# A sub-layer with a gated recurrence and a convolution: the values' projection as a Strassen block product

## What is computed

```
h = rmsnorm(x, pre_norm_g[l])
proj = jnp.einsum('btd,dn->btn', h, w_in[l].astype(h.dtype))
q, fz, iv, gate_a, u, ug, gate_b = jnp.split(proj, split_pts, axis=-1)
o_a = hgrn2_mixer(q, fz, iv, lower_bounds[l], hg_norm_g[l]) * jax.nn.silu(gate_a)
o_b = conformer_conv(u, ug, dw_kernel[l], dw_bias[l], conv_ln_g[l], conv_ln_b[l]) * jax.nn.silu(gate_b)
mixed = jnp.concatenate([o_a, o_b], axis=-1)
y = jnp.einsum('btm,md->btd', mixed, w_out[l].astype(mixed.dtype))
x = x + rmsnorm(y, post_norm_g[l])
```

## Time and profile before

| | |
|---|---|
| median of 3 runs | 869.82 us (869.69 to 869.93) |
| the profiled execution | 869.98 us, of which the span of the page is 868.3 us |
| TensorE busy | 856.2 us, 99% |
| VectorE busy | 628.1 us, 72% |
| ScalarE busy | 413.7 us, 48% |
| GpSimd busy | 330.9 us, 38% |
| moved | 100.27 MB |

### The profile page before, as it was taken

How to read it: one execution, slowest core, us unless ns; L and a number is a source line. 1 busy time by engine, 2 the same in 40 slices (tenths; PEclk the granted TensorE clock), 3 DMA queues, 4 the chain that set the end, 5 groups by cost and what they waited for, 6 DMA issues and landing times.

```text
span 868.3 us, 12325 instructions
## 1 busy us (share of the span) xinstructions
PE 856.2 (99%) x4210; PEld 718.2 (83%) x4210; DVE 628.1 (72%) x1017; ACT 413.7 (48%) x648; POOL 330.9 (38%) x159
## 2 busy tenths in 40 slices
PE   8999999999999999999999999999999999999996
PEld 7988888888888888888888888888888888888885
DVE  4687787787787994775839477583957894686657
ACT  7533313313313465654746466465646843554542
POOL 3294444444444444352442425244342455032100
PEclk9999999999999999999999999999999999999999
DMA  9243333333333323142231313313241246977955
GB/s 309 86 146 97 97 97 97 98 97 97 97 98 97 96 74 97 49 122 73 72 97 52 117 48 99 95 51 104 62 121 48 74 137 210 230 144 158 274 204 194
DMA packets 121342, 100.27 MB, mean 115 GB/s; under 512 B 2992, under 2 KB 101593, under 8 KB 120025
## 3 DMA queue, kind: packets, MB, share of 16 engines
q1 hardware_dynamic: 116201, 86.14, 32.4%
q0 software_dynamic: 4352, 8.39, 5.6%
q10 hardware_dynamic: 752, 5.25, 1.5%
HBM read 95.57 MB, written 4.19 MB: 115 GB/s over the span
## 4 chain that ended last, share of the span: by engine, by line
PE 97%; DMA 1%; ACT 1%; DVE 0%; SPq 0%; DVEq 0%; issue 0%; ACTq 0%
PE banks L1424 19%; PE banks L1422 19%; PE banks L1423 19%; PE banks L1561 3%; PE banks L1560 3%; PE banks L1439 3%; PE banks L1559 3%; PE banks L1438 3%; PE banks L1437 3%; PE banks L1596 3%; PE banks L1595 3%; PE banks L1594 3%; PE banks L1368 3%; PE banks L1480 1%; PE banks L1470 1%; PE banks L1486 1%
## 5 line engine op out<-in xcount | busy, mean ns | idle before, releaser
L426 POOL TENSOR_TENSOR w_lo<-w_raw,w_hi 128x1024 fp32r<-128x1024 f32 x122 | 305.5, 2507 | 419.8 <-ACT w_hi L506 411.8
L1422 PE MATMUL banks<-h_hi,w_hi 128*128 128x512 f32 x736 | 291.1, 396 | 0.0
L1424 PE MATMUL banks<-h_hi,w_lo 128*128 128x512 f32 x736 | 286.7, 390 | 0.0
L1423 PE MATMUL banks<-h_lo,w_hi 128*128 128x512 f32 x736 | 286.5, 389 | 0.0
L506 ACT ACTIVATE w_hi<-w_raw 128x1024 fp32r<-128x1024 f32 x120 | 126.4, 1054 | 168.6 <-PE banks L1424 81.3
L921 DVE SCALAR_TENSOR_TENSOR banks<-work,tap,banks 128x512 f32<-128x512 f32 x232 | 175.3, 756 | 8.0
L1424 PEld LDWEIGHTS banks<-h_hi,w_lo 128*128 128x128 f32 x736 | 138.2, 188 | 29.1
L1423 PEld LDWEIGHTS banks<-h_lo,w_hi 128*128 128x128 f32 x736 | 138.3, 188 | 28.2 <-issue 0.5
L1422 PEld LDWEIGHTS banks<-h_hi,w_hi 128*128 128x128 f32 x736 | 138.3, 188 | 28.0 <-issue 0.5
L1559 PE MATMUL banks<-w_hi,h_hi 128*128 128x512 f32 x128 | 50.8, 397 | 0.0
L1561 PE MATMUL banks<-w_hi,h_lo 128*128 128x512 f32 x128 | 49.9, 390 | 0.0
(11 more groups left out here) (210 smaller groups left out, 1266.3 us busy)
## 6 DMA issues: line engine op xcount, KB each, us to landing
w_raw<-in_w_in SPq DMA_DIRECT2D x112, 512.0 KB, 3.7
w_raw<-in_w_out SPq DMA_DIRECT2D x32, 512.0 KB, 4.9
work<-in_w_out POOLq DMA_DIRECT2D x12, 512.0 KB, 11.5
mix<-in_x ACTq DMA_DIRECT2D x4, 1024.0 KB, 10.4
out_y<-mix SPq DMA_DIRECT2D x3, 1024.0 KB, 3.9
...
```

Of the source, the lines that this page charges most:

```text
L426: g.tensor_tensor(w_lo[:, a], w_raw[:, a], w_hi[:, a].bitcast(fp32), ALU.subtract).then_inc(lo_done, 1)
L1422: mm(bank(b), wh, hh, start=kt == 0, stop=False)
L1423: mm(bank(b), wh, hl, start=False, stop=False)
L1424: ins = mm(bank(b), wl, hh, start=False, stop=kt == KT - 1)
```

## The change

The values' product (512 tokens x 2048 by 2048 x 1024) is cut into 2 x 2 blocks on each side and made from seven block products P1 to P7 in place of eight, as in the output stage. Each has four units, u = 0 to 3, of 256 rows of weights x 512 columns, against 256 tokens: 12 matmuls (`value_products`, `block_products`). The conv stage has 60 units now: 4 + 28 of the convolution and 28 of the values, in turn (ug, V, ug, V, u, V, u, V), P1 beside channel group 1, then P2, P5, P6, P7, P3; in group 7 the four conv units come first and P4's four behind them.

- P5, P6, P7 and P3 need sums of token blocks. GpSimd makes them in 36 operations of 128 x 512 (`v_sum`, in `work`), placed behind its subtractions. ScalarE rounds each side (16 times), VectorE makes the remainder (`v_side_rest`).
- The weights of P5, P6 and P4 are sums built in `gates`: SP loads the first summand, 12 adding transfers issued by GpSimd add the others (`v_add_weights`). P7's weights are formed by VectorE from that sum and a loaded block (`v_third_sum`, 4 times 128 x 1024).
- Results are joined: ScalarE copies P1 (to two places) and P5, VectorE joins the rest (`v_join`), two of the operations from `mix` to `mix`.
- The taps are dealt anew by the table `TAPS_AT`; the loops of VectorE and of GpSimd in this stage are written out.

```diff
-    CONV_T, HEAD_T = 3, 4
-    CONV_U, HEAD_U = 2 * CONV_T, 2 * HEAD_T
-    N_HEAD = J * CONV_U
+    HEAD_U = 8
+    V_STEPS = [(kind, u) for kind in ("P1", "P2", "P5", "P6", "P7", "P3", "P4") for u in range(KT // 4)]
+    UNITS = [("UG", 0, 0), ("UG", 0, 1), ("U", 0, 0), ("U", 0, 1)]
+    for j in range(1, J):
+        conv = [(name, j, half) for name in ("UG", "U") for half in range(2)]
+        vals_now = [("V",) + step for step in V_STEPS[4 * (j - 1):4 * j]]
+        UNITS += conv + vals_now if j == J - 1 else [unit for both in zip(conv, vals_now) for unit in both]
+    N_HEAD = len(UNITS)
+    UNIT_AT = {unit: n for n, unit in enumerate(UNITS)}
+    SUMMED_IN_PLACE = ("P5", "P6", "P4")
+    V_LOADS = [n for n, unit in enumerate(UNITS) if unit[1] not in SUMMED_IN_PLACE]
+    V_RAW = {n: r for r, n in enumerate(V_LOADS)}
+    NO_RAW = N_HEAD - len(V_LOADS)
...
+    V_SUMS = [("P5", part, u) for part in range(3) for u in range(KT // 4)]
+    V_SUMS += [(kind, part, u) for kind in ("P6", "P7", "P3") for u in range(KT // 4) for part in range(2)]
+    V_SUM_DONE = {done: i + 1 for i, done in enumerate(V_SUMS)}
+    V_SUMS_AFTER = {}
+    for i, done in enumerate(V_SUMS):
+        V_SUMS_AFTER.setdefault(i + 8 if done[0] == "P5" else
+                                UNIT_AT["V", done[0], done[2]] - 6 + done[1], []).append(done)
+    ADDS_AFTER = {}
+    for u in range(KT // 4):
+        ADDS_AFTER[10 + 2 * u] = ("P5", u)
+        ADDS_AFTER[UNIT_AT["V", "P5", u] + 1] = ("P6", u)
+        ADDS_AFTER[UNIT_AT["V", "P7", u] + 3] = ("P4", u)
+    BSUM_AFTER = {8 + u: u for u in range(KT // 4)}
+    V_JOINED = {"c11": 2, "u2": 4, "u4": 6, "u3": 10, "c12": 12, "c21": 14}
+    TAPS_AT = {}
+    def share_taps(j, first, counts):
+        w = 0
+        for s, k in enumerate(counts):
+            TAPS_AT.setdefault(first + s, []).append((j, w, w + k))
+            w += k
+    for j in range(J):
+        share_taps(j, UNIT_AT["U", j, 1] + 1, (5, 3, 6, 3, 6, 3, 5) if j == 0 else (1, 6, 3, 6, 2, 6, 2, 5)
+                   if j < J - 2 else (2, 7, 7, 8, 7) if j == J - 2 else (2, 3, 3, 3))
...
+            def v_lo_unit(n, u):
+                pool.wait_ge(hi_done, n + 1)
+                a = slice(n % RING * UW, (n % RING + 1) * UW)
+                g.tensor_tensor(w_lo[:, a], v_bsum[u], w_hi[:, a].bitcast(fp32), ALU.subtract).then_inc(lo_done, 1)
+            def v_sum(kind, step, u):
+                lo, hi, to = 2 * u, KT // 2 + 2 * u, v_first[u] if kind in ("P5", "P6") else v_then[u]
+                if step:
+                    pool.wait_ge(v_summed, V_SUM_DONE[kind, step - 1, u])
+                to = of_side(to)
+                if kind == "P5":
+                    if step == 0:
+                        pool.wait_ge(x_lo, 2 * KT)
+                        pool.wait_ge(par_t, 1)
+                        ins = g.tensor_tensor(to, later(lo, h_hi).bitcast(fp32), later(hi, h_hi).bitcast(fp32), ALU.subtract)
+                    elif step == 1:
+                        ins = g.tensor_tensor(to, to, later(lo, h_lo).bitcast(fp32), ALU.add)
+                    else:
+                        ins = g.tensor_tensor(to, to, later(hi, h_lo).bitcast(fp32), ALU.subtract)
+                elif step == 0:
+                    src, minus = {"P6": (early(lo, h_hi), v_first[u]), "P7": (later(hi, h_hi), v_first[u]),
+                                  "P3": (early(hi, h_hi), v_first[u])}[kind]
+                    if kind in ("P6", "P3"):
+                        pool.wait_ge(v_side_los, V_SIDE["P5" if kind == "P6" else "P7", u] + 1)
+                    if kind == "P7":
+                        pool.wait_ge(v_summed, V_SUM_DONE["P6", 1, u])
+                    ins = g.tensor_tensor(to, src.bitcast(fp32), of_side(minus), ALU.subtract)
+                else:
+                    src = {"P6": early(lo, h_lo), "P7": later(hi, h_lo), "P3": early(hi, h_lo)}[kind]
+                    ins = g.tensor_tensor(to, to, src.bitcast(fp32), ALU.add)
+                ins.then_inc(v_summed, 1)
...
+            for n in range(RING, N_HEAD):
+                if n in V_RAW:
+                    lo_unit(n, n % RING, V_RAW[n] % RING)
+                else:
+                    v_lo_unit(n, UNITS[n][2])
                 if 4 <= n < 10:
                     link(mask_step(n - 4, False))
                     link(mask_step(n - 4, True))
-            g.memset(probs, 0.0).then_inc(masks_ready, 1)
-            with pool.Fori(PEEL, N_FAST // RING) as i:
+                if n == 12:
+                    g.memset(probs, 0.0).then_inc(masks_ready, 1)
+                if n in ADDS_AFTER:
+                    v_add_weights(*ADDS_AFTER[n])
+                for done in V_SUMS_AFTER.get(n, ()):
+                    v_sum(*done)
...
+            def v_side_rounded(kind, u):
+                i = V_SIDE[kind, u]
+                act.wait_ge(v_summed, V_SUM_DONE[kind, 2 if kind == "P5" else 1, u])
+                if i >= SIDES:
+                    act.wait_ge(unit_done, UNIT_AT[("V",) + V_STEPS[8 + i - SIDES]] + 1)
+                A(side_hi[i % SIDES], (v_first if kind in ("P5", "P6") else v_then)[u], ACT.Copy).then_inc(v_side_his, 1)
...
+            def v_third_sum(u):
+                r = V_RAW[UNIT_AT["V", "P7", u]]
+                dve.wait_ge(raw_in[r % RING], 16 * (r // RING + 1))
+                dve.wait_ge(v_added[u], V_LANDED["P6"])
+                V.tensor_tensor(v_raw("P7", u), v_bsum[u], v_raw("P7", u), ALU.subtract).then_inc(v_third, 1)
+            def v_side_rest(kind, u):
+                i = V_SIDE[kind, u]
+                dve.wait_ge(v_side_his, i + 1)
+                V.tensor_tensor(side_lo[i % SIDES], (v_first if kind in ("P5", "P6") else v_then)[u],
+                                side_hi[i % SIDES].bitcast(fp32), ALU.subtract).then_inc(v_side_los, 1)
+            def v_join(kind, b, out, pair, joins=0, op=ALU.add):
+                dve.wait_ge(unit_done, UNIT_AT["V", kind, 3] + 1)
+                if joins:
+                    dve.wait_ge(v_joined, joins)
+                for n in range(2):
+                    V.tensor_tensor(v_block(*out, n), by_head(bank(b + n)), v_block(*pair, n), op).then_inc(v_joined, 1)
...
+            for s in range(2, N_HEAD):
+                before = UNITS[s - 1]
+                if s + 3 < N_HEAD and UNITS[s + 3][:2] == ("V", "P7"):
+                    v_third_sum(UNITS[s + 3][2])
+                if s + 2 < N_HEAD and UNITS[s + 2][1:] in V_SIDE:
+                    v_side_rest(*UNITS[s + 2][1:])
+                if before[0] == "UG" and before[2] == 1:
+                    dve.wait_ge(ug_s, 3 * (before[1] + 1))
+                    V.scalar_tensor_tensor(glu, bank(0), 0.0, glu, ALU.min, ALU.subtract).then_inc(ug_taken, 1)
+                if before[0] == "U" and before[2] == 1:
+                    j, r = before[1], before[1] % 2
+                    dve.wait_ge(glu_ready, j + 1)
+                    dve.wait_ge(unit_done, s)
+                    V.tensor_tensor(apad[r][:, TAPS - 1:], bank(1), glu, ALU.mult).then_inc(u_taken, 1)
+                    V.tensor_copy(tap[:, r * (TAPS + 1):(r + 1) * (TAPS + 1)], par3[:, 0:TAPS + 1, j]).then_inc(tap_ready, 1)
+                    dve.wait_ge(u_taken, j + 1)
+                    dve.wait_ge(tap_ready, j + 1)
+                if before == ("V", "P2", 3):
+                    dve.wait_ge(v_kept, 2)
+                    v_join("P2", 6, C11, C11)
+                if before == ("V", "P6", 3):
+                    dve.wait_ge(v_kept, 4)
+                    v_join("P6", 6, C21, C21, op=ALU.subtract)
+                    dve.wait_ge(v_kept, 6)
+                    dve.wait_ge(v_joined, V_JOINED["u2"])
+                    for n in range(2):
+                        V.tensor_tensor(v_block(*C12, n), v_block(*C12, n), v_block(*C21, n), ALU.add).then_inc(v_joined, 1)
+                if before == ("V", "P7", 3):
+                    v_join("P7", 4, C22, C12, V_JOINED["u4"])
+                    v_join("P7", 4, C21, C21)
+                if before == ("V", "P3", 3):
+                    v_join("P3", 6, C12, C12)
+                for j, a, b in TAPS_AT.get(s, ()):
+                    conv_taps(j, j % 2, a, b)
+                    if b == TAPS:
+                        add_to_sum(j, j == 0)
...
-            def project_values(n, slot, vu):
+            def value_products(kind, u, n):
                 pe.wait_ge(lo_done, n + 1)
-                for tt in range(TT):
-                    o = bank(4 + tt)[:, 0:VW]
-                    for k in range(VK):
-                        a = slice((VK * vu + k) * T + tt * P, (VK * vu + k) * T + (tt + 1) * P)
-                        w = slice(slot * UW + k * VW, slot * UW + (k + 1) * VW)
-                        mm(o, h_hi[:, a], w_hi[:, w], start=vu == 0 and k == 0, stop=False)
-                        mm(o, h_hi[:, a], w_lo[:, w], start=False, stop=False)
```

(16 more changed lines are left out.)

273 lines of the change are left out of this document (147 added, 126 removed).

## The result

The changed kernel takes **915.25 us** (median of 4 runs, 912.26 to 920.17) against 869.88 of the kernel before beside it: 1.0526 times as long, with a 95% interval of 1.0471 to 1.0581. That is 45 us slower. The forecast had the sign and not the size; the time lies far above the range.

A forecast was written before the change was run, and what follows sets the result against it. TensorE, busy 99%, was taken to bound the kernel: -10.9 for fewer matmuls, +14.1 waiting for VectorE, +2.4 behind f_v, sum +5.6 on 869.98, forecast 875.6 us. Own range 872 to 881; 8 in 10, 862 to 884.

The forecast's parts named there:

- So the first kind waits for the running GpSimd instruction, less 0.15 or so: VectorE operations with both inputs in SBUF wait only for the one GpSimd instruction running; 0.93 us per meeting on average.
- the price of 16.7 us: Held VectorE operations from channel 4's glu to f_v: 12.5 us for 20 meetings plus 4.2 for three direct followers.
- counting from channel 4: VectorE's work counted from channel 4's glu to the first head's two results (f_v): 134.2 us plus 2.0, TensorE 138.8.
- the bound of 48: Upper bound on VectorE's waiting in the counted stretch: 23 held operations at 2.08 us each.
- the 2.08 us for one operation: Waiting part of a 2.77 us VectorE operation, both inputs in SBUF, started 0.41 us after a GpSimd subtraction began.
- 48 matmuls at an unchanged pace, -10.9: TensorE: 16 value units of 24 matmuls replaced by 28 of 12, 48 fewer at 0.2267 us, -10.9 us.
- GpSimd's sum of 512: GpSimd's token sum of half a subtraction's size: taken as 1.25 us, bounds 1.20 and 2.40.
- Its end behind unit 18's subtraction: GpSimd done with units 5 to 18 at 101.1, 1.0 us before TensorE starts unit 18; costs nothing.
- The transfers land in time: Adding transfers for block weights have 24.5 us until P6's first is rounded; longest landing 15.0 us.
- the waits for sides and for the first head's products: TensorE waits 14.1 us for VectorE, for side remainders of P7 and P3 and before head unit 4.
- Rival 3: GpSimd becomes the bound, TensorE waiting for weights' low parts from unit 16: 8 to 10 us, 884; chance 0.08.
- the exclusive lock for the whole instruction: Skill's rule for the port shared by VectorE and GpSimd: wait about 19 us, time 2 us more than forecast.

The follow-up runs named there:

- experiment 9: Changed kernel without tap copies, channel sums 0 to 5 from PSUM, P7's weights by transfer, masks later, GpSimd waiting for itself behind weight subtractions only: 866.22 us.

## Why the prediction was wrong

- **The step that failed** is "So the first kind waits for the running GpSimd instruction, less 0.15 or so", and with it the price of 16.7 us. It holds for most operations and not for all: the copy at 78.76 and the channel sums at 166.16 and 255.27 stood 24.1, 10.5 and 9.3 us, 44 of the 73 us that all held operations lost. The rows it rested on the earlier trace rows showed a GpSimd that idled before and behind the pair in question, where both theories give the same number. Nor did I see that the stretch was too short: counting from channel 4 left out the copy at 78.76, half a stage earlier and the longest hold of all. Between 45 and 350 us the held groups take 73 us more than their operations need alone: copies 31.5 - 8 x 0.17 = 30.1, sums 26.0 - 6 x 0.69 = 21.9, sides 28.5 - 16 x 0.68 = 17.6, joins 4.6 - 1.4 = 3.2, third sums next to nothing (5.0 - 4.8).
- In the stretch that the forecast did count (from 195.25, the glu of channel 4, to f_v at 352) the held operations lost 25.9 us where it had 16.7, and the channel sum at 255.27 alone is the difference. That the others come to 16.6 is partly luck: the third sums were hardly held (0.2 us), copies and joins more than their share. The sum stayed under the bound of 48, but the 2.08 us for one operation that it was made of did not hold. The number to read was the length of GpSimd's row from an operation to the next real wait; the order of GpSimd's instructions was known, and so was that its waits were already satisfied.
- **Missing altogether**: the granted clock. I counted standing time alone, and of the 60.9 us lost 19.7 are slower running after a stop.
- **Right**: 48 matmuls at an unchanged pace, -10.9 (experiment 9 shows TensorE's busy time 9.1 shorter). GpSimd's sum of 512, taken as 1.25, is 1.29. Its end behind unit 18's subtraction, forecast at 101.1, is 101.24, which is luck in part: unit 5's subtraction began 2 us later than taken (47.3), and the issue of a transfer took 0.8 us of the row in place of 1.21. The taps are immune. The transfers land in time in the changed kernel (7.6 us in the middle). VectorE is the engine that decides, and the waits for sides and for the first head's products are there, larger: 8.1 + 14.8 + 3.2 = 26.1 us where 14.1 was forecast. Of the 13.2 beside them, 11.0 came by way of the glu and ScalarE, which I had named as standing behind VectorE and then priced at nothing.
- **Rival 3**, GpSimd as the bound, was not what happened (of TensorE's 15.7 us of waits for `w_lo`, 11.0 came by way of a late rounding), but it was what came next: with broken rows TensorE waited for `w_lo`, and a token sum with its wait costs 1.4 us.
- Of the Trainium skill (SBUF — State Buffer, "Who interferes with whom") the forecast named the exclusive lock for the whole instruction. The short holds agree (2.66 us at 202.04); the long ones show more than that: 24.3 and 20.3 us across many instructions. Its caution about moving work between VectorE and GpSimd (Perfetto Trace Analysis, "Optimizing Scalar/DVE Operations") was not tested as such, since no run has the token sums on VectorE; what the runs show is that GpSimd's token sums beside VectorE's new operations turned a saving of 10.9 us into a loss of 45.
